# Double-buffered Q and K tiles, and the next head's Q/K projection issued inside attention, in a fused encoder-layer kernel

## The reference, cut to what matters

```python
logits = einsum('bqhmd,bkhmd->bhmqk', q, k2) * ATT_SCALE + bias   # m = 0, 1: two softmax maps per head
a = softmax(where(mask, logits, NEG_INF))
wts = a[:, :, 0] - lam * a[:, :, 1]
o = einsum('bhqk,bkhe->bqhe', wts, v)
o = rmsnorm(o, g_subln) * (1.0 - lambda_init)
```

## Time and profile before

| what | us |
|---|---|
| median of 3 runs (lowest, highest) | 2640.48 (2637.74, 2937.14) |
| the profiled execution | 2635.82 |
| its span on core 6, the slowest | 2634.8 |
| spans of the 8 cores | 2612.5 to 2634.8 |
| first Q matmul of head 0, last sum matmul (L1062) of head 7 | 305.55, 1377.72 |

### The profile page before, as it was taken

One profiled execution on the slowest core, in us unless ns is written; L12 is line 12 of the kernel. 1 busy time (PEld: TensorE's weight loads), 2 busy tenths in 40 slices (PEclk: granted clock), 3 DMA queues, 4 the chain that ended last, 5 costly groups with the idle time before them and its releaser, 6 DMA issues.

```text
span 2634.8 us, 40673 instructions; the slowest of 8 cores (2612.5 to 2634.8 us)
## 1 busy us (share of the span) xinstructions
PE 2200.4 (84%) x14928; PEld 1216.0 (46%) x15112; DVE 950.4 (36%) x1322; ACT 705.4 (27%) x1200; POOL 196.3 (7%) x264
## 2 busy tenths in 40 slices
PE   3328588888787878797878969999999999999995
PEld 1214253636363626362626845544454454444442
DVE  4503325251515151615252241224314413422438
ACT  3502245353626262626260050000000000000003
POOL 0010100202020202010101000000000000000000
PEclk9999888999899999988998969999999999999998
DMA  5985440606070707060729526444444544444403
GB/s 161 217 124 51 62 58 27 76 27 76 11 92 1 101 1 102 1 94 1 154 84 134 76 40 89 65 64 65 65 65 65 74 71 75 71 65 65 65 1 144
DMA packets 287817, 189.50 MB, mean 72 GB/s; under 512 B 143009, under 2 KB 269729, under 8 KB 281663
## 3 DMA queue, kind: packets, MB, share of 16 engines
q0 software_dynamic: 248480, 122.45, 36.5%
q1 hardware_dynamic: 39144, 64.44, 8.3%
HBM read 279.39 MB, written 29.84 MB: 117 GB/s over the span
## 4 chain that ended last, share of the span: by engine, by line
PE 69%; DVE 13%; ACT 7%; issue 4%; DMA 3%; another core or an unknown queue 1%; DVEq 1%; ACTq 0%; POOL 0%; SPq 0%; POOLq 0%
PE bank L1189 13%; PE bank L1192 13%; PE bank L1220 11%; PE bank L713 7%; PE bank L683 5%; PE bank L1127 4%; PE bank L1060 3%; PE bank L1062 3%; ACT pt L226 3%; PE bank L1044 3%; PE bank L527 3%; DVE tmpn L226 2%; DVE post_r L226 2%; DVE hres L226 2%; DMA xs<-xin 2%
## 5 line engine op out<-in xcount | busy, mean ns | idle before, releaser
L1189 PE MATMUL bank<-n2T,wgu 128*128 128x512 bf16 (+1 forms) x2078 | 363.2, 326 | 5.9 <-issue 2.4
L226 DVE TENSOR_TENSOR hres<-bank,hres 128x512 f32<-128x512 f32 (+1 forms) x468 | 304.6, 651 | 168.4 <-PE bank L1127 102.9
L1192 PE MATMUL bank<-n2T,wgu 128*128 128x512 bf16 (+1 forms) x2068 | 362.3, 325 | 2.3
L1220 PE MATMUL bank<-wd,actT 128*128 128x512 bf16 x1551 | 344.3, 380 | 12.2 <-DVE hres L226 10.4
L226 ACT ACTIVATE sgt<-bank 128x512 f32<-128x512 f32 x132 | 64.8, 491 | 900.1 <-PE bank L1192 899.1
L226 DVE TENSOR_TENSOR actT<-bank,sgt 128x512 bf16<-128x512 f32 x132 | 73.7, 558 | 623.3 <-ACT sgt L226 623.3
L1189 PEld LDWEIGHTS bank<-n2T,wgu 128*128 128x128 bf16 x2112 | 178.8, 98 | 177.5 <-issue 10.2
L1192 PEld LDWEIGHTS bank<-n2T,wgu 128*128 128x128 bf16 x2112 | 178.9, 98 | 166.2
L1220 PEld LDWEIGHTS bank<-wd,actT 128*128 128x128 bf16 x1584 | 154.6, 98 | 197.4 <-issue 16.7
L1060 PE MATMUL bank<-pt,Vb 128*128 128x512 bf16 (+1 forms) x464 | 195.7, 422 | 46.7 <-ACT pt L226 34.1
L226 ACT ACTIVATE pt<-bank,cols 128x512 bf16<-128x512 f32 (+1 forms) x304 | 208.8, 687 | 53.7 <-PE bank L1044 30.2
(11 more groups left out here) (136 smaller groups left out, 1616.9 us busy)
## 6 DMA issues: line engine op xcount, KB each, us to landing
wgu<-w_gate POOLq DMA_DIRECT2D x22, 1024.0 KB, 9.3
wgu<-w_up POOLq DMA_DIRECT2D x22, 1024.0 KB, 13.5
wd<-w_down POOLq DMA_DIRECT2D x11, 2048.0 KB, 12.6
xs<-xin SPq DMA_DIRECT2D x17, 1024.0 KB, 6.7
w<-w_in POOLq DMA_DIRECT2D x32, 512.0 KB, 15.1
rscr<-r8d POOLq DMA_DIRECT2D x8, 1288.0 KB, 55.2
bown<-rscr SPq DMA_DIRECT2D x8, 1280.0 KB, 7.3
y<-hres SPq DMA_DIRECT2D x9, 1024.0 KB, 3.9
```

What stands on the lines that cost most here:

```text
L226: return f(*a, **k)
L1189: nc.tensor.matmul(bA.f32[:, 0:n], lhsT=sl.t[:, c, 0, sub * 128:(sub + 1) * 128], rhs=n2T[:, c, c0:c0 + n], start=(c == 0), stop=(c == 15))
L1192: tk = nc.tensor.matmul(bB.f32[:, 0:n], lhsT=sl.t[:, c, 1, sub * 128:(sub + 1) * 128], rhs=n2T[:, c, c0:c0 + n], start=(c == 0), stop=(c = ...
L1220: tk = nc.tensor.matmul(bk.f32[:, :], lhsT=actT[g % 2][:, i, tt * 128:(tt + 1) * 128], rhs=sl.t[:, i, cb * 512:(cb + 1) * 512], start=(i = ...
```

## The change

There are now two tiles each for transposed Q and K (`QT2`, `KT2`), by the parity of the head. `proj_T` and `proj_tok` become generators that give up after each group of matmuls. `inproj_qk_gen` strings the Q and K projections of one head together; head 0's runs ahead of the loop, and that of head h+1 is pulled piece by piece (`pull_nxt`) inside head h's attention: at every third step, where `pull` is called. These projections take their bank from `ringS`, and all their copies out of PSUM are DVE's. Only the V projection is left in front of a head's attention, and the second part of the last post stands behind it. To make room, the weight ring has 3 slots (4 before), and the two `ktm` tiles become one: the second sample's keys are loaded after `sample_prep(0)` has read the first's, and `sample_prep(1)` becomes a piece of the filler. The order of the rest, the bias loads and masks at the start of each head among it, stays.

```diff
-    NW = 4
+    NW = 3
...
-    QT = mem.alloc("QT", [128, 2, NQ], BF16)
-    KT = mem.alloc("KT", [128, NTOK], BF16)
+    QT2 = [mem.alloc(f"QT{i}", [128, 2, NQ], BF16) for i in range(2)]
+    KT2 = [mem.alloc(f"KT{i}", [128, NTOK], BF16) for i in range(2)]
...
-        cslots.append(dict(ktm=mem.alloc(f"ktm{i}", [128, 17, 128], BF16), kcT=mem.alloc(f"kcT{i}", [128, 2064], BF16),
+        cslots.append(dict(kcT=mem.alloc(f"kcT{i}", [128, 2064], BF16),
                            vc=mem.alloc(f"vc{i}", [128, 17, 128], BF16), ds=newdsem(f"d_c{i}"), free=[], ready=None))
+    ktm = mem.alloc("ktm", [128, 17, 128], BF16)
+    ktm_ds = newdsem("d_ktm")
+    ktm_free = []
...
+    def proj_T_gen(sl, groups, dstT, is_q, dve_only, ring, wait_free):
+        res = {"last": None, "toks": []}
         for (c0, n, dst0) in groups:
-            bk = ringP.next()
-            PE.wait(sl.ready, bk.free, qkv_free)
+            bk = ring.next()
+            PE.wait(sl.ready, bk.free, wait_free)
             for c in range(16):
...
+            res["last"] = last
+            if is_q:
+                if dve_only:
+                    DVE.wait(last, t_qz)
+                    ta_ = DVE(nv.tensor_copy(out=dstT[0:64, 0, dst0:dst0 + n], in_=bk.f32[0:64, 0:n]))
+                    te = DVE(nv.tensor_copy(out=dstT[64:128, 1, dst0:dst0 + n], in_=bk.f32[64:128, 0:n]))
+                else:
...
+            elif dve_only:
+                DVE.wait(last)
+                te = DVE(nv.tensor_copy(out=dstT[:, dst0:dst0 + n], in_=bk.f32[:, 0:n]))
...
+            res["toks"].append(te)
+            yield res
+        yield res
...
+        def st_copy(out, in_, waits):
+            if dve_only:
+                DVE.wait(waits)
+                return DVE(nv.tensor_copy(out=out, in_=in_))
+            ACT.wait(waits)
+            return ACT(ns.copy(out=out, in_=in_))
...
+            yield res
+        bk = ring.next()
+        PE.wait(sl.ready, bk.free, wait_free)
...
+    def inproj_qk_gen(hh, dve_only, ring):
+        par = hh % 2
+        wi_ = 8 + 3 * hh
+        toks = []
+        sl_ = w_get(wi_)
+        r = None
+        for r in proj_T_gen(sl_, [(0, 512, 0), (512, 512, 512), (C_SAMP, 128, 1024)], QT2[par], True, dve_only, ring,
+                            buf_free[par]):
+            yield
+        toks += r["toks"]
+        w_release(wi_, r["last"])
+        sl_ = w_get(wi_ + 1)
+        for r in proj_T_gen(sl_, [(0, 512, 0), (512, 512, 512), (1024, 512, 1024), (1536, 512, 1536),
+                                  (2048, 160, 2048)], KT2[par], False, dve_only, ring, buf_free[par]):
+            yield
+        toks += r["toks"]
+        for r in proj_tok_gen(sl_, hh, k_o, False, dve_only, ring, []):
+            yield
+        w_release(wi_ + 1, r["last"])
+        qk_ready[hh] = toks
+
+    run_gen(inproj_qk_gen(0, False, ringP))
...
+        QT, KT = QT2[h % 2], KT2[h % 2]
         rb = h * 128 * LTOT
         SP.wait(t_rscr, bias_free)
...
         t_bias = [t_bias_ld, t_mask]
+        def load_cache_k(s):
+            POOL.wait(ktm_free)
+            ktm_ds.inc(ng.dma_start(out=ktm[:, 0:16, :],
+                                    in_=ck_v[s, 0:2048, h, :].rearrange("(t p) d -> p t d", p=128)))
+            return ktm_ds.inc(ng.dma_start(out=ktm[0:16, 16, :], in_=ck_v[s, 2048:2064, h, :]))
+
+        ktm_ready = {0: load_cache_k(0)}
         for s in range(2):
             cs = cslots[s]
             POOL.wait(cs["free"])
-            for (src, dst) in ((ck_v, cs["ktm"]), (cv_v, cs["vc"])):
-                cs["ds"].inc(ng.dma_start(out=dst[:, 0:16, :],
-                                                 in_=src[s, 0:2048, h, :].rearrange("(t p) d -> p t d", p=128)))
-                cs["ds"].inc(ng.dma_start(out=dst[0:16, 16, :], in_=src[s, 2048:2064, h, :]))
+            cs["ds"].inc(ng.dma_start(out=cs["vc"][:, 0:16, :],
+                                      in_=cv_v[s, 0:2048, h, :].rearrange("(t p) d -> p t d", p=128)))
+            cs["ds"].inc(ng.dma_start(out=cs["vc"][0:16, 16, :], in_=cv_v[s, 2048:2064, h, :]))
             cs["ready"] = cs["ds"].total
...
         wi = 8 + 3 * h
-        sl = w_get(wi)
-        lastq, tq = proj_T(sl, [(0, 512, 0), (512, 512, 512), (C_SAMP, 128, 1024)], QT)
-        w_release(wi, lastq)
+        sl = w_get(wi + 2)
+        r = run_gen(proj_tok_gen(sl, h, v_o, True, False, ringP, []))
+        lastv, tv = r["last"], r["toks"]
+        w_release(wi + 2, lastv)
         if carry:
             carry.pop()()
-        sl = w_get(wi + 1)
-        lastk, tkT = proj_T(sl, [(0, 512, 0), (512, 512, 512), (1024, 512, 1024), (1536, 512, 1536),
-                                 (2048, 160, 2048)], KT)
-        lastk2, _ = proj_tok(sl, h, k_o, False)
-        w_release(wi + 1, lastk2)
-        sl = w_get(wi + 2)
-        lastv, tv = proj_tok(sl, h, v_o, True)
-        w_release(wi + 2, lastv)
-        qkv_ready = tq + tkT + tv
+        qkv_ready = qk_ready[h] + tv
...
+        def sample_prep(s):
+            nonlocal ktm_free
+            cs = cslots[s]
+            qb = Qbd[s]
+            DVE.wait(qkv_ready, qbd_free[s])
...
+                PE.wait(ktm_ready[s], bk.free, cs["free"])
...
+            ktm_free = [PE.last]
+            samp_prep[s] = (t_qbd, t_kcT)
...
@@ -905,6 +959,9 @@
                 cs = cslots[s]
                 qb = Qbd[s]
                 p0 = 64 * s
+                if s == 1:
+                    sample_prep(1)
+                    yield
...
-                PE.wait(pts_toks, SAcc.free)
+                PE.wait(pts_toks, SAcc.free, cs["ready"])
...
-        sample_prep()
+        sample_prep(0)
+        ktm_ready[1] = load_cache_k(1)
         filler = sample_gen()
+        nxt = inproj_qk_gen(h + 1, True, ringS) if h + 1 < nheads else None
+
+        def pull_nxt():
+            if nxt is not None:
+                try:
+                    next(nxt)
+                except StopIteration:
+                    pass
...
                 tk_pv = stageB(*steps[i - 2])
                 if B == 0 or i >= 14:
                     pull()
+                    if i % 3 == 0:
+                        pull_nxt()
...
                                          512, h, abT[:, 8 + h, q0:q0 + 512], tk_pv, acc))
         while pull():
             pass
+        if nxt is not None:
+            run_gen(nxt)
         carry.append(deferred.pop())
-        qkv_free = [PE.last] + [samp_prep[s_][0] for s_ in range(2)]
+        buf_free[h % 2] = [PE.last] + [samp_prep[s_][0] for s_ in range(2)]
         bias_free = [PE.last, DVE.last, ACT.last]
```

More of the change, by code:

```diff
@@ L719, in proj_tok @@
                 ks = kst_next()
-                ACT.wait(last, ks.ds.total, ks.free)
-                te = ACT(ns.copy(out=ks.t[:].rearrange("p a b -> p (a b)"), in_=bk.f32[:, :]))
+                te = st_copy(ks.t[:].rearrange("p a b -> p (a b)"), bk.f32[:, :], [last, ks.ds.total, ks.free])
                 rd.append(te)
```

79 lines of the change are left out of this document (36 added, 43 removed).

## The result

The changed kernel takes 2727.36 us (median; 2725.53 to 2731.95), 1.0332 times the time before, with a 95% interval of 1.0318 to 1.0346: slower by 3.3%, where 2660 and "within 2%" were forecast, and 2 us outside the range.

A forecast was written before the change was run, and what follows sets the result against it. PE was taken as full in the projections and loose in attention. Seven heads' growth of 17.8 (124.6), six gains of 17.5 (-105.0) and the last head's +3.5 gave +23 us on 2635.8: 2659, stated as 2660, range 2600 to 2725.

The forecast's parts named there:

- Sum covered: 7.0: Block B=0: waits, DVE/ACT catching up and regained clock would absorb 7.0 of the 22.7 us of groups.
- Part 2: Attention in heads 0 to 6: taking in 31.8 us of projections, it would grow by 17.8 us a head.
- the 2.5 us set against it: Block B=0: cost of held banks, the second sample's preparation in the filler and late bias adds, 2.5 us.
- the forecast's own sign: Attention in the new profile: expected 97 to 101 us in heads 0 to 6; above 104 us, covering failed.
- the waits it named: Block B=0: PE waits of 1.3 and 1.2 us covered wholly, and about half of one of 2.0 us.
- The clock at the start: Start of each attention: half clock after the idle behind V costs nothing new, since 903 to 909 is slow already.
- The 2.0 us taken back late in B=0: Stretch from 936 to 940, at half clock with gaps: dense groups ahead of it would win back 2 us.
- B=1 was to grow by 2.1: Block B=1: 9.1 us of groups, less 3.5 and 0.8 covered and 2.7 of clock taken back.
- Head 0's projections are as before: Head 0, ahead of attention: its projections would take the same time as before, with no cost.
- Part 1: Ahead of attention: the load chain to `ktm` sets the start at +36.2 us, a gain of 17.5 a head.
- The last head: Last head: attention 1.5 us shorter, 5 us lost as `ktm` lands at about +59 behind `hres`; +3.5 in all.
- A: Rival for attention: groups not covered, ACT and DVE run dry; growth 33 us a head, 2766 us; chance 0.22.

The follow-up runs named there:

- Experiment 2: The changed kernel with half of the contraction left out in every Q and K group inside attention: 2625.7 and 2627.3 us.
- experiment 1: The changed kernel without the Q and K projections of heads 1 to 7, all heads using head 0's Q and K: 2537.13 us, ratio to before 0.9601.
- Experiment 8: The changed kernel with head 0's Q and K projections written behind its bias and cache loads: 2721.37 us, ratio to before 1.0247.
- Experiment 5: The changed kernel with cached keys and values issued in POOL's queue ahead of the bias wait and masks: 2661.34 us, ratio to before 1.0074.
- experiment 3: The kernel of experiment 6 with the groups ahead of attention, banks from all eight, most copies on ACT: 2630.39 us, ratio to before 0.9941.
- experiment 6: The kernel of experiment 5 with bias loads waiting only for DVE's last bias add, not the whole post part: 2624.29 us, ratio to before 0.9925.
- experiment 7: The kernel before the change, with bias loads waiting only for DVE's last bias add: 2639.65 us, ratio to before 0.9965.
- experiment 4: The changed kernel with 64 unread matmuls of 512 columns put behind V in heads 1 to 7: 2733.01 us, ratio to before 1.0341.
- experiment 12: The changed kernel, groups whole, with early cache loads, early bias release, head 0's loads first, last head's big loads behind second sample's keys: 2602.85 us, ratio to before 0.982.

## Why the prediction was wrong

**What failed is the step "Sum covered: 7.0" of Part 2,** with the 2.5 us set against it. B=0 was to grow by 22.7 - 7.0 + 2.5 = 18.2 us and grew by 26.0: 1.7 for the second sample's transposes (said: 1.5) and 24.3 for the groups, where 16.7 was left for them. Of these 24.3 some 2 us are slow clock (time at 1.2 GHz in the block is 7.2 us a head without groups and 10.9 with them), so about 22 us were paid for 22.7 of work. By the forecast's own sign, attention above 104 us, covering failed: it is 108.8. Yet the waits it named did shrink: in PE's timeline of head 3 the products of the sample's near keys and the first post matmul stand without a wait (1.3 and 1.2 us in the earlier trace rows), and the third was 1.34 us of 1.98.

```profile
817.10 3.61 PE L686 MATMUL bank<-xnT,w 128*128 128x512 bf16 x16
...
821.29 0.23 PE L1016 MATMUL bank<-pts,Vb 64*128 64x128 bf16 x1
...
834.22 0.19 PE L1046 MATMUL bank<-spost_q,ones_b 128*128 128x64 bf16 x1
```

The fault was to book them as a net gain. A group goes ahead of the next score product on PE, so ACT and DVE get their next piece a group later; when PE comes back, they have as little work done ahead as before, and it waits anew. Experiment 2 shows this as 10.6, 10.0 and 10.8 us idle, and the rows around one group there show DVE and ACT standing still and the wait behind. That every wait comes back in this way is argued: it fits all runs, and the rows show it for one group.

**The clock at the start "costs nothing new" was wrong too.** The first group stands in the slow stretch, where before only short work stood: 4.81 to 6.25 us in heads 0 to 6, 5.7 on the mean, against 3.61, so 2.1 us a head and some 15 us in all; in four heads a later group of B=0 was slow too, up to 6.34 us. That the slow stretch would stay was said; what would newly lie in it wasn't asked. By the rule cited there (the Trainium skill, "TensorE: Matmul & The Clock Gate", Part 1: an idle gap halves the array's clock) the trace agrees: 0.50 from 942 to 947, behind the gap. The 2.0 us taken back late in B=0 did not come on balance: in the kernel before that stretch was slow in four heads of eight only (0.79 over the last 8 us of B=0, else 1.00), it is at 0.97 to 1.00 now, but the time at 1.2 GHz in the whole block rose from 9.2 to 10.9 us a head.

**B=1** was to grow by 2.1 and grew by 4.6. (The forecast split head 4 at 940.4; the marks used here split it at 942.5, which moves 2.1 us between the blocks and changes neither growth.) Both of its terms were right in kind and too large. The wait for `spost_q` went, as said, but PE's idle time fell from 5.8 to 3.1 us a head, 2.7 where 4.3 (3.5 + 0.8) were said. The clock came back, as said, but 2.7 us were taken from head 4, where it was 0.66 over the first 10 us; in six of the eight heads it was 0.83. Time at 1.2 GHz fell from 6.3 to 2.4 us a head, which leaves 1.8 us. The block in head 4, before, and then without groups (experiment 1); the changed kernel's is the fourth window of the section on the result:

```profile
942.50:977.20 34.70, 28.94 (x112) 9.52 (x114) 18.24 (x21) 23.95 (x38) 0.00 (x0) 0.90 0.00 1
```

```profile
871.50:906.50 35.00, 30.69 (x121) 10.52 (x122) 18.04 (x21) 23.94 (x38) 0.00 (x0) 0.85 0.00 1
```

**"Head 0's projections are as before" was wrong by 12 us.** They stand ahead of the bias loads now, and with them their `kout` stores, on SP's own queue:

```profile
332.85 3.96 SPq L745 DMA_DIRECT2D kout<-kst  x2
...
339.29 0.43 SPq L880 DMA_DIRECT2D bown<-rscr  x1
```

The masks come at 353.7, `ktm` is issued at 357.2, the transposes start at 367.0. The order showed it; I didn't follow it for head 0. Experiment 8 takes them back.

**Right:** the gap. Part 1 gave -17.5 a head and it was -18.7: the bias chain holds `ktm`, at +12, +24.4 and +28 where +12, +22.9 and +26.5 stood, and PE idles 18.6 us for it. Experiment 5 found that this chain has a second arm, through POOL's casts into `Vb`. The start of attention was -3.3 (said -2.5). The last head was +3.9 (said +3.5), with `ktm` landing late behind `hres` as said and the transposes at +55.9 where +59 stood. That the sum agrees is luck: the gap gave +2.3 of the 5 said, attention grew by 1.6 where it was to shrink by 1.5, and over the eight cores the gap is anything from 49.6 to 57.6.

```profile
ktm<-ck POOLq DMA_DIRECT2D x1, 512.0 KB, 27.4
```

**The rivals.** A named what happened, ACT and DVE running dry in a group, and where it decides (a growth of 22 us), but its end of 33 was not reached: 27. By the forecast's own sum 27.1 a head, with 12 for head 0, gives 7 x 27.1 - 105 + 3.5 + 12 = +100. Its chance of 0.22 was too low: the evidence against it was four waits that a group could stand in, and they say where idle time is, not that it stays away. The Trainium skill ("Perfetto Trace Analysis", Optimization Strategy) says that interleaving regimes with different busiest engines may help. Here the runs do not bear that out: inside attention or ahead of it, a head takes the same within 2 us (experiments 3 and 6).

**Still open:** whether the four edits of the best version would speed up the kernel before as well, where only one was tried (experiment 7); and whether more score banks in flight would let ACT work on through a group; the accumulators and the ring of three use all eight banks, and it wasn't tried.

## What to carry to other kernels

Idle time made of many short waits on a chain through other engines is no room for PE's own work: filling one wait makes the next, unless the chain has work queued to go on with. Measure that before building an interleave: leave the moved work out, put half of it in, and see whether the idle time shrinks. Look at the clock of each stretch beside it: here B=1 seemed to cover half its groups, and most of that was the clock. When dense work leaves a place, ask which load chain it hid, and what stands ahead of that chain in the queues of SP and POOL; here the gain of 1.8% came from four such edits (cache loads first, bias buffers back early, head 0's loads first, the residual last), on top of the change.

## What the runs showed of the hardware

In experiment 4 a gap of 4.95 us behind some 30 us of unbroken matmuls (V, then the added products, clock 1.00) was followed by a granted clock of 0.50: 16 transposes took 1.86 us. I had expected that much dense work to carry over it. In head 6 of the same run there was no gap over 1.13 us, but PE was busy only 2.2 of the 4.7 us up to the first product with V, and the clock behind them was 0.55.

A 512 KB load issued while 9 MB and 1 MB are on their way took 27.4 to 35.5 us to land, where it takes 6.7 in the last head of experiment 12; its landing came about with theirs (30.5 and 35.4).
